# Adaptive-norm conditioning computed beside three FFNs instead of two, with its VectorE steps cut into small shares

## The reference, cut to what matters

```python
def reference(x, c, ctx, c_ctx, w_ada, b_ada, ...):        # D = 1024, 512 latent + 256 context tokens
    x = x + _pos_2d(L, x.dtype)[None]; xc = ctx
    for l in range(2):
        mod_lat = (silu(c) @ w_ada[l] + b_ada[l]).reshape(b, 9, D)       # w_ada[l]: 1024 x 9216
        mod_ctx = (silu(c_ctx) @ w_ada[l] + b_ada[l]).reshape(1, 9, D)
        x  = _post(x,  _swiglu(_pre(x,  g[0], mod_lat, 0), ffn1_gu[l], ffn1_down[l]), g[1], mod_lat, 0, 0.5)
        xc = ...                                            # the same with mod_ctx
        x, xc = mixer(...)                                  # S5 heads and FNet heads, modulated by mod[3:6]
        x  = _post(x,  _swiglu(_pre(x,  g[4], mod_lat, 2), ffn2_gu[l], ffn2_down[l]), g[5], mod_lat, 2, 0.5)
    return x                                                # _swiglu: (silu(gate) * up) @ w_down, D_FF = 2816
```

## Time and profile before

| what | value |
|---|---|
| three runs | 2861.47, 2871.16, 2871.52 us, median 2871.16 |
| profiled execution, first to last instruction (its span; no other time is given for it) | 2864.4 us |
| mean granted TensorE clock | 0.969 |
| TensorE matmuls busy | 2680.7 us, 94% of the span |
| VectorE / ScalarE / GpSimd busy | 1677.3 / 716.3 / 821.0 us |
| f10, f20, f11, f21 | about 67 to 692, 1009 to 1594, 1630 to 2205, 2470 to 2837 us |

### The profile page before, as it was taken

How to read it: one execution, slowest core, us unless ns; L and a number is a source line. 1 busy time by engine, 2 the same in 40 slices (tenths; PEclk the granted TensorE clock), 3 DMA queues, 4 the chain that set the end, 5 groups by cost and what they waited for, 6 DMA issues and landing times.

```text
span 2864.4 us, 39514 instructions
## 1 busy us (share of the span) xinstructions
PE 2680.7 (94%) x16446; PEld 2496.0 (87%) x16446; DVE 1677.3 (59%) x2235; ACT 716.3 (25%) x977; POOL 821.0 (29%) x1292
## 2 busy tenths in 40 slices
PE   5899999998899889999999799999998898899996
PEld 4899999997869789999999699999998766588885
DVE  5868877865582686766665743343434683644444
ACT  4211121113413421111111322112122413322222
POOL 1258775732050200000000228767551050100001
PEclk9999999999999999999999899999999999899998
DMA  9443444442455134343441232222233455133321
GB/s 314 125 132 125 152 152 128 129 165 87 151 147 162 45 111 125 111 130 114 132 126 52 74 74 87 95 94 89 94 103 120 138 167 161 57 96 99 96 89 59
DMA packets 340459, 337.09 MB, mean 118 GB/s; under 512 B 52529, under 2 KB 311225, under 8 KB 336697
## 3 DMA queue, kind: packets, MB, share of 16 engines
q1 hardware_dynamic: 279224, 204.07, 24.3%
q10 hardware_dynamic: 51840, 77.07, 8.0%
q0 software_dynamic: 9216, 53.42, 5.0%
HBM read 290.02 MB, written 44.50 MB: 117 GB/s over the span
## 4 chain that ended last, share of the span: by engine, by line
PE 81%; DVE 11%; ACT 3%; DMA 2%; issue 2%; SPq 1%; POOL 0%; DVEq 0%; ACTq 0%; POOLq 0%
PE ps L454 71%; DVE adaW L541 3%; PE ps L1390 2%; PE ps L582 2%; PE ps L1089 2%; ACT wH L439 1%; PE ps L1415 1%; DVE tmpN L1168 1%; DMA y_d<-YC 1%; DVE wL L446 1%; DVE rmsX L1177 1%; DVE xT L1049 1%; PE ps L1404 1%; DMA xin<-in_x_dram 1%; PE ps L1074 1%
## 5 line engine op out<-in xcount | busy, mean ns | idle before, releaser
L454 PE MATMUL ps<-hH,wH 128*128 128x384 f32 (+1 forms) x2928 | 1019.9, 348 | 67.9 <-DVE hL L1186 48.1
L454 PE MATMUL ps<-hL,wH 128*128 128x384 f32 (+1 forms) x2928 | 1011.6, 345 | 0.0
L454 PE MATMUL ps<-hH,wL 128*128 128x384 f32 (+1 forms) x2928 | 1010.9, 345 | 0.0
L446 DVE TENSOR_TENSOR wL<-raw,wH 128x1024 fp32r<-128x1024 f32 x300 | 392.0, 1319 | 551.9 <-ACT wH L439 551.3
L454 PEld LDWEIGHTS ps<-hH,wH 128*128 128x128 f32 x2928 | 556.1, 190 | 95.6 <-issue 55.9
L454 PEld LDWEIGHTS ps<-hL,wH 128*128 128x128 f32 x2928 | 556.3, 190 | 18.1
L454 PEld LDWEIGHTS ps<-hH,wL 128*128 128x128 f32 x2928 | 555.5, 190 | 18.5
L454 PE MATMUL ps<-midH,wH 128*128 128x384 f32 (+1 forms) x1232 | 426.2, 346 | 12.7 <-DVE wL L446 9.9
L454 PE MATMUL ps<-midH,wL 128*128 128x384 f32 (+1 forms) x1232 | 423.6, 344 | 0.0
L454 PE MATMUL ps<-midL,wH 128*128 128x384 f32 (+1 forms) x1232 | 423.2, 344 | 0.0
L439 ACT ACTIVATE wH<-raw 128x1024 fp32r<-128x1024 f32 x300 | 310.8, 1050 | 448.2 <-PE ps L454 399.3
(11 more groups left out here) (257 smaller groups left out, 2382.3 us busy)
## 6 DMA issues: line engine op xcount, KB each, us to landing
raw<-in_ffn_gu_dram SPq DMA_DIRECT2D x176, 512.0 KB, 3.8
adaW<-in_w_ada_dram ACTq DMA_DIRECT2D x40, 1536.0 KB, 7.0
raw<-in_ffn_down_dram SPq DMA_DIRECT2D x88, 512.0 KB, 3.7
x_d<-xT POOLq DMA_DIRECT2D x4, 3072.0 KB, 9.6
xT<-x_d POOLq DMA_DIRECT2D x4, 3072.0 KB, 11.1
W_d<-gW POOLq DMA_DIRECT2D x16, 512.0 KB, 4.0
VT_d<-gVT ACTq DMA_DIRECT2D x16, 512.0 KB, 3.0
raw<-in_w_in_dram SPq DMA_DIRECT2D x16, 512.0 KB, 6.2
```

Of the source, the lines that this page charges most:

```text
L446: nc.vector.tensor_tensor(wL[:, n % SPLIT_SLOTS, :], raw[:, n % RAW_SLOTS, :], wH[:, n % SPLIT_SLOTS, :].bitcast(f32), ALU.subtract).then_ ...
L454: ins = nc.tensor.matmul(dst, a, b, start=first and n == 0, stop=last and n == 3 * len(pairs) - 1)
```

## The change

Rides 8 to 47 are dealt over three FFNs: f10 gets 14 (8 to 21), f20 gets 12 (22 to 33), f11 gets 14 (34 to 47). Their 16 steps each are no longer done in blocks of 16 or 8: the FFN's steps are cut by a table of shares over "hooks", four ahead of the loop and twelve in each period. Hook 0 stands behind VectorE's `split_lo` of the unit three ahead of gate unit 0, hook 1 behind `up` of unit 1, hook 2 behind the next `split_lo`, hook 3 behind `up` of unit 3, hooks 4 to 11 each behind one addition to `yT`. `place_rides` puts a ride's column sums ahead of the first free unit (s, i), gate or up, for which all 16 steps stand in hooks up to i - 1 of the period (or, for i = 0, in the period before). ScalarE's `up` can take a ride's columns now, and TensorE waits for `ada_taken` before it reuses such a tile's slot.

```diff
+    STEPS = 2 * KC
+    HOOK_SHARES = (4, 4, 4, 4) + (1,) * KC
+    LEAD_SHARES = (0, 0, 2, 4)
+    def share_after(s, hook):
+        if s < 0:
+            return sum(LEAD_SHARES[:hook + 1])
+        return sum(LEAD_SHARES) + s * sum(HOOK_SHARES) + sum(HOOK_SHARES[:hook + 1])
+    def share_before_unit(s, i):
+        return share_after(s, i - 1) if i else share_after(s, -1)
+    LAST_SHARE = share_before_unit(NPH - 2, 3)
+    def steps_due(n_rides, share):
+        return min(STEPS * n_rides, STEPS * n_rides * share // LAST_SHARE)
+    def place_rides(rides):
+        units = [(s, i) for s in range(NPH - 1) for i in range(4)]
+        at = {}
+        for k, R in enumerate(rides):
+            at[next(u for u in units if steps_due(len(rides), share_before_unit(*u)) >= STEPS * (k + 1) and u not in at)] = R
+        return at
...
-    F1_0 = make_ffn("f10", 0, ffn1_gu, ffn1_down, 0, 8, True)
+    F1_0 = make_ffn("f10", 0, ffn1_gu, ffn1_down, 0, range(8, 22), True)
-    F2_0 = make_ffn("f20", 0, ffn2_gu, ffn2_down, 0, 28, False)
-    F1_1 = make_ffn("f11", 1, ffn1_gu, ffn1_down, 0, None, True)
+    F2_0 = make_ffn("f20", 0, ffn2_gu, ffn2_down, 0, range(22, 34), False)
+    F1_1 = make_ffn("f11", 1, ffn1_gu, ffn1_down, 0, range(34, 48), True)
...
 ffn_tensor:
+        ride_in = {4 + 12 * s + i: R for (s, i), R in F.ride_of.items()}
+        def free_tile(g):
+            if g >= F.slots:
+                wait_tile(pe, F, g - F.slots)
+            if g - F.slots in ride_in:
+                pe.wait_ge(ada_taken, ride_in[g - F.slots] + 1)
...
-                ride = F.ride0 + 2 * s + i // 2 if F.ride0 is not None and i % 2 == 0 else None
-                gate_up(4 + 6 * s + i, 4 + 12 * s + i, ride)
+                gate_up(4 + 6 * s + i, 4 + 12 * s + i, F.ride_of.get((s, i)))
 ffn_scalar:
-        def up(i, f):
+        def up(i, g, f, ride):
             act.wait_ge(up_read, F.n0["up_read"] + f + 1)
+            take_ride(g, ride)
 ffn_vector:
+        def ada_until(s, hook):
+            if not F.rides:
+                return
+            n = len(F.rides)
+            for step in range(steps_due(n, share_after(s, hook - 1)), steps_due(n, share_after(s, hook))):
+                ada_step_of(dve, F.rides[step // STEPS], step % STEPS)
...
         for s in range(NPH - 1):
-            more = F.ride0 is not None and s < NPH - 2
-            if F.ride0 is not None:
-                ada_steps(dve, F.ride0 + 2 * s + 1, 0, STEPS)
             for j in range(2):
                 i, g, f = 4 + 6 * s + 2 * j, 4 + 12 * s + 2 * j, 2 + 2 * s + j
-                if j and more:
-                    ada_steps(dve, F.ride0 + 2 * s + 2, 0, KC)
                 split_lo(dve, F.base + i + 3)
+                ada_until(s, 2 * j)
                 up(i + 1, g + 1, f)
-            down(8 + 6 * s, 8 + 12 * s, s, F.ride0 + 2 * s + 2 if more else None)
+                ada_until(s, 2 * j + 1)
+            down(8 + 6 * s, 8 + 12 * s, s)
```

More of the change, by code:

```diff
@@ L338, in make_spill, with make_ffn @@
         return made["spill"]
-    def make_ffn(tag, layer, gu, down, tok0, ride0, gen):
+    def make_ffn(tag, layer, gu, down, tok0, rides, gen):
         nonlocal unit
         F = Section("ffn", FFN_COUNTS)
-        F.tag, F.layer, F.tok0, F.ride0, F.base = tag, layer, tok0, ride0, unit
+        F.tag, F.layer, F.tok0, F.base = tag, layer, tok0, unit
+        F.rides = rides
+        F.ride_of = place_rides(rides)
         unit += 6 * (FC // 2)
@@ L381, in build @@
     pre_first.sq = sq_first
-    F1_0 = make_ffn("f10", 0, ffn1_gu, ffn1_down, 0, 8, True)
+    F1_0 = make_ffn("f10", 0, ffn1_gu, ffn1_down, 0, range(8, 22), True)
     M0 = make_mixer("m0", 0, F1_0.gen)
-    F2_0 = make_ffn("f20", 0, ffn2_gu, ffn2_down, 0, 28, False)
-    F1_1 = make_ffn("f11", 1, ffn1_gu, ffn1_down, 0, None, True)
+    F2_0 = make_ffn("f20", 0, ffn2_gu, ffn2_down, 0, range(22, 34), False)
+    F1_1 = make_ffn("f11", 1, ffn1_gu, ffn1_down, 0, range(34, 48), True)
     M1 = make_mixer("m1", 1, F1_1.gen)
-    F2_1 = make_ffn("f21", 1, ffn2_gu, ffn2_down, CTX, None, False)
+    F2_1 = make_ffn("f21", 1, ffn2_gu, ffn2_down, CTX, range(0), False)
     plan = []
@@ L510, in build @@
     FIRST_RIDES = 8
-    FFN_RIDES = 20
     def ada_source(layer, ride_in_layer):
@@ L519, in ada_dma, with ada_step_of @@
         act.dma_start(adaW[:, R % 2, :, :], ada_source(*divmod(R, RIDES))).then_inc(ada_ready[R % 2], 16)
-    STEPS = 2 * KC
-    def ada_steps(dve, R, first, last):
+    def ada_step_of(dve, R, i):
         before = STEPS * (R - FIRST_RIDES)
         w = adaW[:, R % 2]
[L528 to L542, removed]
+        k, v = i // 2, 1 - i % 2
+        needed = before + (i if i < 4 else i - 1)
+        if needed:
+            dve.wait_ge(ada_step, needed)
+        if i == 0:
+            dve.wait_ge(ada_ready[R % 2], 16 * ((R - FIRST_RIDES) // 2 + 1))
+            ins = nc.vector.tensor_scalar(adaP[:], w[:, 0], siluC[:, 0, 0:1], None, ALU.mult)
+        elif i == 1:
+            ins = nc.vector.tensor_scalar(w[:, 0], w[:, 0], siluC[:, 0, 1:2], None, ALU.mult)
+        else:
+            at = w[:, 1 - v]
+            ins = nc.vector.scalar_tensor_tensor(at, w[:, k], siluC[:, k, v:v + 1], adaP[:] if i == 3 else at, ALU.mult,
+                                                 ALU.add)
+        ins.then_inc(ada_step, 1)
     def ada_ride(pe, R, bank, col):
@@ L612, in ffn_tensor, with gate_up @@
     def ffn_tensor(pe, F, pre):
-        def gate_up(i, g, ride):
+        ride_in = {4 + 12 * s + i: R for (s, i), R in F.ride_of.items()}
+        def free_tile(g):
             if g >= F.slots:
                 wait_tile(pe, F, g - F.slots)
+            if g - F.slots in ride_in:
+                pe.wait_ge(ada_taken, ride_in[g - F.slots] + 1)
+        def gate_up(i, g, ride):
+            free_tile(g)
             if ride is not None:
@@ L631, in down @@
             for m in range(KC):
-                wait_tile(pe, F, g + m - F.slots)
+                free_tile(g + m)
                 for h, (t0, w) in enumerate(halves(F.tok0)):
@@ L671, in next_ride, with take_ride @@
         def next_ride(R):
-            if R < F.ride0 + FFN_RIDES:
+            if R in F.rides:
                 ada_dma(act, R)
-        if F.ride0 is not None:
[L677 to L683, removed]
+        def take_ride(g, ride):
             if ride is not None:
@@ L686, in gate @@
                 next_ride(ride + 2)
+        if F.rides:
+            act.wait_ge(h_lo, KC * F.pre.nth + KC)
+            next_ride(F.rides[0])
+            next_ride(F.rides[0] + 1)
+        def gate(i, g, f, ride):
+            act.wait_ge(w_used, F.base + i + 1)
+            take_ride(g, ride)
             if f >= 2:
@@ L700, in ffn_scalar @@
             gate(2 * j, 2 * j, j, None)
-            up(2 * j + 1, j)
+            up(2 * j + 1, 2 * j + 1, j, None)
         for s in range(NPH - 1):
             for j in range(2):
-                i, f = 4 + 6 * s + 2 * j, 2 + 2 * s + j
-                gate(i, 4 + 12 * s + 2 * j, f, None if F.ride0 is None else F.ride0 + 2 * s + j)
-                up(i + 1, f)
+                i, g, f = 4 + 6 * s + 2 * j, 4 + 12 * s + 2 * j, 2 + 2 * s + j
+                gate(i, g, f, F.ride_of.get((s, 2 * j)))
+                up(i + 1, g + 1, f, F.ride_of.get((s, 2 * j + 1)))
             piece = s - 1 if F.gen and 1 <= s <= PIECES else None
@@ L735, in up, with down @@
                                     midH[:, f % 4, F.tok0:TOK].bitcast(f32), ALU.subtract).then_inc(mid_lo, 1)
-        def down(i, g, p, ride=None):
+        def ada_until(s, hook):
[4 more added lines that the diff above has]
+                ada_step_of(dve, F.rides[step // STEPS], step % STEPS)
+        def down(i, g, p):
             for m in range(KC):
-                if ride is not None:
-                    ada_steps(dve, ride, KC + m, KC + m + 1)
                 if m < KC - 1:
@@ L748, in down @@
                                         sb_pair(yT[:, m, :], F.tok0), ALU.add).then_inc(down_read, 1)
+                if p < NPH - 1:
+                    ada_until(p, 4 + m)
             if p < NPH - 1:
@@ L753, in ffn_vector @@
         for j in range(2):
-            if F.ride0 is not None:
-                ada_steps(dve, F.ride0, j * KC, (j + 1) * KC)
             split_lo(dve, F.base + 2 * j + 3)
+            ada_until(-1, 2 * j)
             up(2 * j + 1, 2 * j + 1, j)
+            ada_until(-1, 2 * j + 1)
         for s in range(NPH - 1):
-            more = F.ride0 is not None and s < NPH - 2
-            if F.ride0 is not None:
-                ada_steps(dve, F.ride0 + 2 * s + 1, 0, STEPS)
             for j in range(2):
                 i, g, f = 4 + 6 * s + 2 * j, 4 + 12 * s + 2 * j, 2 + 2 * s + j
-                if j and more:
-                    ada_steps(dve, F.ride0 + 2 * s + 2, 0, KC)
                 split_lo(dve, F.base + i + 3)
+                ada_until(s, 2 * j)
                 up(i + 1, g + 1, f)
```

(3 more changed lines are left out.)

## The result

The changed kernel takes **3066.8 us** (median of 4 runs, 3065.8 to 3068.0) against 2870.0 us (median of 4): a ratio of 1.070, 95% interval 1.068 to 1.071. The forecast was slower, 3055 us, range 3000 to 3108. By span it is 3064.8 against 2864.4 us, 200.4 us more, where the sum had said 184.

The account below looks back on a forecast made before the run. The prediction took TensorE's matmuls plus its waits to bound the kernel. Terms -27 + 125 + 54 + 32 = +184 us on a span of 2864.4 gave 3048, with 6.8 from span to median 3055 us, range 3000 to 3108.

Parts of the forecast that it names:

- Part 1: Fewer rides in f10: it can lose its 26.1 us of excess and f20 its 0.5, -27 us.
- Part 2: TensorE waits ahead of column sums for each ride's last step in f10, f20 and f11: 114.5 us in 23 waits.
- the walk through the shares: Counting due steps hook by hook to find each ride's last step: 41.5 us each in f10 and f11, 31.5 in f20.
- Part 3: GpSimd slows VectorE's steps at hook 0 in f10 and f11: +10 us, making the ride waits 125.
- 3.18 + 0.53 p: Forecast TensorE wait in us for a ride whose last step is the p-th of hook 0 or 2.
- Part 4: Lowered clock behind each new ride wait: 2.4 us for 22, 1.5 for one, +54 us, bounds 33 and 75.
- Part 5: Hook 3's steps delay the first `yT` addition in nine periods each of f10 and f11: +32 us, 25 to 59.
- The clock stays up: Rival: the waits come, but TensorE's clock does not fall behind them: 3001 us, chance 0.06.
- GpSimd slows every step: Rival: all steps in f10 and f11 are slowed, not only hook 0's: some 3110 us, chance 0.09.
- The steps are there in time: Rival: no ride waits, only the -27 us acts: 2844 us, or 2860 with half of Part 5, chance 0.05.

Follow-up runs that it names:

- e5: As e2, but with column sums ahead of gate tiles (units 0 and 2) only: 2839.6 us, ratio 0.991 to the kernel before.
- e1: The changed kernel with every ride's sums one unit later, deal and sums ahead of up tiles kept: 2879.0 us, ratio 1.004 to the kernel before.
- e4: The changed kernel with overwritten filler matmuls ahead of the column sums, keeping TensorE at work while it waits for a ride: 3002.7 us, ratio 1.047 to before.
- e2: As e1, but no steps in hook 3, ahead of the first `yT` addition (shares 5, 5, 6, 0): 2839.9 us, ratio 0.991 to before.
- e7: The kernel before with only its rides dealt 14, 12, 14 over three FFNs, still in blocks, two per period: 2885.6 us, ratio 1.006 to before.
- e6: As e2, but the 40 rides dealt over two FFNs (20, 20, 0): 2899.8 us, ratio 1.012 to the kernel before.
- e8: As e6, but with 18, 18 and 4 rides: 2844.1 us, ratio 0.992 to the kernel before.

## Why the prediction was right, point by point

**What bounds, and how.** Right: the extra time is TensorE's waits and the clock behind them.

**Part 1, what can go (-27 us).** By e5 the three FFNs with next to no ride or `yT` waits take 1761.0 us, 23.1 less than before. Right in kind; I had put all of f10's excess down to stops with the sums at 1.23 us each. By e5 a ride adds about 1.5: its 14 rides lengthen f10 to 595.0, while f11 without rides is 574.6 with 1.6 us of slow clock in its last units, so (595.0 - 573.0) / 14 = 1.57, of which 0.1 is the 1.3 us of ride waits that e5 still has in f10.

**Part 2, the ride waits (114.5 us).** Right in place, number and size: 23 waits, in the units that the walk through the shares named. f20, with GpSimd quiet, was forecast at 31.5 us and measured at 31.5. That the place of the sums is the cause is shown by e1, which moves nothing else but a last share, and saves 188 us. The term for the ride waits was 125 with Part 3 and came out at 122.5.

**Part 3, GpSimd (+10).** f10 and f11 have 45.2 and 45.8 us instead of 41.5: +8.0. The excess is behind hook 0, as argued: in f10 the waits for its rides 8 and 11 (counted from 0) are 5.5 and 6.5 us where 3.18 + 0.53 p gives 3.7 and 4.8, and the one for ride 1, 5.3 us, has none. The four steps of hook 0 above took 4.93 us, those of hook 1 2.19. The remark that all 14 rides of f11 could have been done in f20 was too wide: six of them came from f10, where GpSimd works too.

**Part 4, the clock (+54), the mis-sized term.** The FFNs together are 1990.2 - 1761.0 = 229.2 us longer than e5's; without ride waits (122.5) and `yT` waits (28.0), 78.7 us are left, 3.4 per ride wait and a little above my upper bound of 75. e4 shows some 66 of them to be clock; the other 13 were not taken apart. The mis-sized step is the middle between 1.5 us (behind a wait of 1.2) and 3.35 (behind one of 6.6). By FFN these 78.7 are 27.4 us in f10 and 28.7 in f11 for 8 ride waits, and 22.7 in f20 for 7: 3.4, 3.6 and 3.2 each, though f20's are the shorter ones, 1.7 to 6.1 us. So the price of the long wait fits nearly all of them on average, and 23 x 3.35 would have given 77.

**Part 5, the first `yT` addition (+32).** 28.0 us in 18 waits, nine per FFN with three slots and none in f20, as forecast. e2 shows that waits of this kind are on the path in full, and that the clock costs little behind them, some 5 us behind e1's 18 and not 18 x 1.5 = 27, so the upper bound of 59 was far off.

**The sum.** -23.1 + 122.5 + 78.7 + 28.0 - 5.7 (rest of the kernel) = 200.4 us, the two spans' difference, against a sum of 184: the clock's 25 us too little and the 4 us too much taken off in Part 1 are partly made up by the 2.5 and 4 us too much in the waits and the 5.7 us of the rest. The 6.8 us that were added from span to median are not a property of the kernel: here the median lies 2.0 us over the span. So 3055 is nearer to 3066.8 than the sum deserves, by 5 us of luck.

**The rivals.** "The clock stays up" fell by the windows above and e4. "GpSimd slows every step": the mean step is 734 ns in f10 and 735 in f11, but the slow ones are where hook 0 stands. "The steps are there in time" fell; e2 comes near to that case, at 2840 us where I had said 2844. The Trainium skill (GPSIMD Engine Reference, 1. Specifications) lets GpSimd contend with VectorE instructions of two SBUF inputs. The trace agrees in another row as well: in f11, with GpSimd busy for 322 us, a step's mean is 735 ns and a `wL`, with two SBUF inputs, 1504, against 611 and 1223 in f20, with GpSimd busy for 9 us, while `yT`, with one input in PSUM, takes 952 in both.

**Which part of the change does what.** Sums behind the last hook: -188 us when moved (e1). Steps ahead of `yT`: 34 to 39 us more (e1 against e2). Up tiles: nothing (e5 against e2). The third FFN: a loss of 18 us with blocks (e7), and with fine shares it gives the buffers time: 60 us between 20, 20, 0 and 14, 12, 14 (e6 against e2), all but 4 of them had with four rides in f11 (e8). e2 and e5 beat both kernels, by 27 us and 227 us.

## What to carry to other kernels

When work of a side engine is cut into the gaps of its stream, what counts for the consumer is not how evenly it is spread but behind which wait the last piece stands: count from the consumer's wish back to that wait, and leave one unit of the consumer's work between. Deadlock-free ("all steps are in the stream by then") is the earliest place that works, and was the slower of the two tried here, by 188 us. And slack at the consumer is time that a buffer is held: check what is queued behind the reload on the in-order engine.

## What I had not expected of the hardware

The loss to the slow clock does not go in proportion to the wait. Behind 23 ride waits of 1.7 to 7.3 us what is left besides the waits is 3.4 us each on average, most of it clock by e4; behind the 18 waits of 1.1 to 2.2 us of e1 it is 0.3 us each (38.7 us for 33.6 us of waits), while a ride wait of 1.2 us in the kernel before cost 1.5. In the changed kernel the ride waits are followed at once by the column sums, which TensorE ran in 2.69 us in place of 1.23 in the case shown; the `yT` waits are followed by full matmuls. What decides between the two was not taken apart, nor was the length of the wait held fixed.

A busy filler is cheaper than idling: 639 more matmuls made the kernel 64 us shorter (e4), though nothing that TensorE waits for came sooner.
